# Expert passes of 104 token rows in place of 112, and a fourth round of passes in the general path

## What is computed

```
def swiglu(h, wg, wu, wd):
    return (jax.nn.silu(h @ wg) * (h @ wu)) @ wd

def moe_ffn(h, w_router, wg, wu, wd):
    hf = h.reshape(-1, D_MODEL)                      # 336 x 1024
    logits = (hf @ w_router).astype(jnp.float32)     # 336 x 8
    top_v, top_i = lax.top_k(logits, TOP_K)          # TOP_K = 2
    gates = jax.nn.softmax(top_v, axis=-1)
    ...
    out = jax.ops.segment_sum(yb * row_gate[:, None], row_tok, ...)
```

## Time and profile before

| | before |
|---|---|
| median of 3 runs | 1788.92 us (1786.96 to 1791.72) |
| the profiled execution's own time | 1789.18 us |
| its span, from first to last instruction | 1787.5 us |
| TensorE busy with matmuls | 1675.8 us (94%) |
| TensorE busy with weight loads | 1409.0 us (79%) |
| VectorE, ScalarE, GpSimd busy | 325.3, 210.5, 110.2 us |
| mean granted TensorE clock | 0.939 of full speed |
| bytes moved by DMA | 395.60 MB, mean 221 GB/s |

### The profile page before, as it was taken

One profiled execution on the slowest core, in us unless ns is written; L12 is line 12 of the kernel. 1 busy time (PEld: TensorE's weight loads), 2 busy tenths in 40 slices (PEclk: granted clock), 3 DMA queues, 4 the chain that ended last, 5 costly groups with the idle time before them and its releaser, 6 DMA issues.

```text
span 1787.5 us, 45176 instructions
## 1 busy us (share of the span) xinstructions
PE 1675.8 (94%) x20545; PEld 1409.0 (79%) x20545; DVE 325.3 (18%) x878; ACT 210.5 (12%) x603; POOL 110.2 (6%) x181
## 2 busy tenths in 40 slices
PE   3999889999999999988899999999999999999993
PEld 3767556666666766655699999999999999999993
DVE  1254631000000135552120000100000010000002
ACT  1144101000000014411010000100000000000000
POOL 6020100400000002010010000000000000000001
PEclk8999659999999999966899999999999999999997
DMA  8932112896444332211249999898998989899873
GB/s 169 265 108 86 39 39 94 292 351 230 135 111 117 97 94 66 84 50 32 90 163 341 360 314 383 305 369 325 336 371 293 375 300 360 325 339 383 283 277 103
DMA packets 211077, 395.60 MB, mean 221 GB/s; under 512 B 26466, under 2 KB 88410, under 8 KB 210736
## 3 DMA queue, kind: packets, MB, share of 16 engines
q1 hardware_dynamic: 195504, 346.83, 56.3%
q0 software_dynamic: 15152, 45.88, 8.5%
q10 hardware_dynamic: 240, 0.07, 0.0%
HBM read 357.16 MB, written 37.54 MB: 221 GB/s over the span
## 4 chain that ended last, share of the span: by engine, by line
PE 91%; DVE 4%; DMA 3%; issue 1%; ACT 1%; SPq 0%; POOLq 0%; POOL 0%; DVEq 0%
PE bank L1126 31%; PE bank L1144 15%; PE bank L1031 11%; PE bank L676 6%; PE bank L1048 6%; PE bank L1009 4%; PE bank L637 3%; DMA ring<-in_w_in 2%; PE bank L964 2%; PE bank L975 2%; PE bank L990 1%; PE bank L651 1%; PE bank L605 1%; DVE arena L1690 1%; PE bank L654 1%
## 5 line engine op out<-in xcount | busy, mean ns | idle before, releaser
L1126 PE MATMUL bank<-arena,ring 128*64 128x112 f32 x11264 | 547.3, 259 | 12.3 <-issue 12.2
L1126 PEld LDWEIGHTS bank<-arena,ring 128*64 128x64 f32 x11264 | 540.8, 137 | 17.6 <-issue 16.3
L1144 PE MATMUL bank<-arena,ring 128*64 128x112 f32 x5632 | 274.4, 259 | 1.8 <-issue 1.6
L1144 PEld LDWEIGHTS bank<-arena,ring 128*64 128x64 f32 x5632 | 271.5, 137 | 4.6 <-issue 4.1
L1031 PE MATMUL bank<-hnT,ring 128*128 128x336 f32 x704 | 199.1, 446 | 1.8 <-DVE hnT L1446 1.8
L1031 PEld LDWEIGHTS bank<-hnT,ring 128*128 128x128 f32 x704 | 133.7, 190 | 67.3 <-issue 2.3
L1827 DVE TENSOR_TENSOR arena<-arena,bank 128x112 f32<-128x112 f32 x176 | 47.7, 271 | 513.8 <-ACT arena L1400 513.8
L676 PE MATMUL bank<-hnT,ring 128*128 128x336 f32 x384 | 118.4, 453 | 0.0
L1400 ACT ACTIVATE arena<-bank 128x112 f32<-128x112 f32 x176 | 46.3, 263 | 513.5 <-PE bank L1126 513.5
L1048 PE MATMUL bank<-arena,ring 128*128 128x336 f32 x352 | 99.6, 446 | 0.0
L676 PEld LDWEIGHTS bank<-hnT,ring 128*128 128x128 f32 x384 | 70.0, 190 | 33.8 <-issue 4.6
(11 more groups left out here) (342 smaller groups left out, 1139.6 us busy)
## 6 DMA issues: line engine op xcount, KB each, us to landing
ring<-in_moe_w_gate SPq DMA_DIRECT2D x88, 1024.0 KB, 9.4
ring<-in_moe_w_up SPq DMA_DIRECT2D x88, 1024.0 KB, 8.8
ring<-in_moe_w_down SPq DMA_DIRECT2D x88, 1024.0 KB, 10.0
ring<-in_w_in SPq DMA_DIRECT2D x14, 1024.0 KB, 6.3
ring<-in_w_gate SPq DMA_DIRECT2D x11, 1024.0 KB, 12.8
ring<-in_w_up SPq DMA_DIRECT2D x11, 1024.0 KB, 11.7
xg_rows<-arena POOLq DMA_DIRECT2D x1, 11200.0 KB, 50.5
y_rows<-arena POOLq DMA_DIRECT2D x1, 10752.0 KB, 92.6
```

Source lines behind the costliest of these rows:

```text
L1126: ins = mm(bank[3 + f % 2][rows, SLOTS * w:SLOTS * w + SLOTS], weights[:, col:col + 64], xg[:, c, :], start=(c == 0), stop=(c == DK - 1))
L1144: ins = mm(bank[5 + c // 4][rows, SLOTS * (c % 4):SLOTS * (c % 4) + SLOTS], weights[:, col:col + 64], hid[:, f, :], start=(f == 0 and c % ...
```

## The change

`SLOTS` goes from 112 to 104, and `PASSES` = ceil(336 / `SLOTS`) follows from 3 to 4. Nothing else is edited.

```
-SLOTS = 112
+SLOTS = 104
 PASSES = -(-NT // SLOTS)
```

## The result

| | before | after |
|---|---|---|
| median | 1787.94 us (1785.3 to 1791.72, 4 runs) | 1812.16 us (1811.39 to 1815.6, 4 runs) |
| ratio to before | | 1.0135, 95% interval 1.0121 to 1.015 |
| profiled execution, span | 1787.5 us | 1810.1 us |

What follows compares the result with a forecast made beforehand. TensorE's expert matmuls were taken as the bound, with DMA right behind. Columns -56.3 us, holes +14 us and the rest 0 summed to -42 us against 1789.2 us, giving 1747 us, range 1731 to 1768 us.

Steps and rivals of the forecast that it cites:

- Part 1: Expert matmuls on TensorE: 8 fewer columns in each of 8448 pairs save 56.3 us; a pass without holes takes 96.2 us.
- Rival (c): Expert matmuls: the weight load, not the columns, sets 95.9 ns a pair; 1789 us, no change; chance 0.03.
- Part 2: Expert stage: the fullest expert has exactly 104 rows, so eight passes are enough and the fourth round stays unrun.
- rival (d): Expert stage: one row over 104 enters the general path, 24 more passes run, above 4000 us in all; chance 0.02.
- Part 3: TensorE in the expert stage: late program blocks come later and new ones appear, costing 14 us, bounds nothing to 25 us.
- rival (a): Expert stage: no new holes in TensorE's stream, only the column gain of 56.3 us, so 1733 us; chance 0.14.
- Part 4: Expert weight loads: bytes do not shrink, 364 GB/s needed, the ring helps; no cost taken, 30 us kept for a rival.
- Rival (b): Expert stage: DMA takes over as the bound, a pass lasts 101 us, 1753 to 1775 us in all; chance 0.18.
- Part 5: Edges of a pass and L1088: 128-column sides remain, so no gain taken, 0.3 us at most.
- Part 7: Zero fills: 5.2 MB (23%) more, landing at 437 to 494 us, before ACT's wait at 603.72 us; hidden, no cost.

## Why the prediction was wrong, point by point

**Part 1, the columns: right.** The pass without holes came out at 96.4 us (96.2 forecast) in the run with half the bytes, and 120 slots gave 110.31 (110.27 by the same law). Rival (c) is out.

**Part 2, no fourth round of passes: right.** Counts of 11264 and 5632 as before; rival (d) did not come.

**Part 3, the holes: right mechanism, wrong size.** I took 14 us with an upper bound of 25 (the formula behind it gives 23); the stage loses 65.7 in place of 21.7 us, 44 us more. The term was built as "each of the 25 late blocks is later by 0.43 us, a few new ones are added". That treats the arrival as a scatter with a tail. The rows show something near a floor: while the weights stream, a block comes every 6.2 to 6.4 us. At 112 slots TensorE used one every 6.14 us and stood close to the floor, so few holes were seen, 25. At 5.71 us there are 65, at about half of the stage's 133 block edges. Most of the edges without one follow a pass's start, where the DMA pauses (in the third pass its share is 0.11 from 1166.17 to 1170.17 us): the first 881 matmuls of that pass, nearly seven blocks, run without a hole. I had also miscounted the holes before: five of the eight passes had three or more, not six. The few holes of the kernel before looked like a small problem; they were the sign of a limit just reached. The Trainium skill, "Runtime: NRT & Kernel Launch", section "Instruction fetch mechanics", calls the cost of a block edge mostly hidden. By that, rival (a) would have come. The trace does not agree where TensorE uses a block in less than 6.3 us: 43.2 us of such waits stand in the stage after the change.

**Part 4, weights in the expert stage: right.** TensorE waits for no slab in the stage after the change, and SP still waits 496 us for TensorE. Rival (b) forecast 1753 to 1775 us by a wrong mechanism: the DMA does take gain away, but through the program blocks, not the weights. One reading in this part was loose: rows 8 show the DMA empty for 4 us, not some 8.

**Part 5, L1088: wrong by 2.2 us.** In the kernel before, the granted clock rose from half (1.2 GHz) to full (2.4 GHz) during these 48 matmuls. With 104 or 108 columns it stays at half until the stage has begun. With 112 columns and four rounds, or with 120, it rises as before. First a window of the kernel before, then two after the change, the third number from the end being the clock:

```profile
908.00:910.00 2.00, 2.00 (x20) 2.00 (x20) 0.91 (x2) 0.54 (x1) 1.43 (x2) 0.99 0.91 367
```
```profile
942.00:944.00 2.00, 2.00 (x12) 2.00 (x11) 1.44 (x3) 0.52 (x1) 1.45 (x2) 0.50 0.90 371
944.00:946.00 2.00, 2.00 (x11) 2.00 (x11) 0.00 (x0) 0.00 (x0) 1.63 (x2) 0.50 0.92 363
```

L1088 takes 9.83 us in place of 7.24. What keeps the clock down with fewer columns is not shown.

**Part 7, the fills: the step that turned the sign.** I asked who waits for the fills, found ACT at 603.72 us, and called them hidden. The landing, 171 us after its issue, was even inside what I had allowed (494 us on the clock; it came at 493). Nobody waited for it. This is the step that failed: "Hidden" was concluded from the deadline of the fills alone, and a term of 32.8 us was put at nothing. What I did not ask is who shares the DMA while they run. The feed-forward of layer 0 takes a slab of 1 MB each 9.05 us (32 matmuls of 282.8 ns), and the landing of a gate slab was already up to 53.6 us in the kernel before, against a median of 12.8. During the fills SP got out one slab each 12 us before (six from 343.28 to 416.68 us) and one each 20 us after (seven from 343.16 to 486.28 us), and so for nearly twice as long; the 11 slots of the ring, some 100 us, ran out at 437 us. The 5.2 MB more cost nothing by themselves, as the run with 112 slots and four rounds shows, and the slow layout with fewer bytes cost 5.7 us. Together they outlast the ring, and the price is 32.8 us. I had the thought that the rate might be lower by half, but used it on the landing alone.

Together: -56.3 + 44 (holes) + 32.8 (layer 0) + 2.2 (L1088) = +23 us, against 22.6 in the spans, the small rest being within what the ends of the kernel move from run to run. The fills turned the sign, but part 3 alone would have been enough to miss: with the fills over 128 partitions the kernel takes 1780.36 us, and the forecast went from 1731 to 1768.

## What to carry to other kernels

A background transfer is hidden only if those who share the DMA with it have room too: ask for its rate, how long it lasts at that rate, and its neighbours, not only for its deadline. Keep the outer dimension of a big DMA apart from tuning constants, near 128 partitions: here 104 and 120 cost about 100 GB/s against 112 and 150 against 128, and repairing that turned a kernel 1.4% slower into one 0.5 to 0.7% faster. Where an engine shows a few unexplained waits at even distances of instructions, compare its pace with the distance: if they are near each other, a faster engine will meet a floor and not a scatter.

## What was not expected of the hardware

- The DMA rate while a fill runs beside the weight loads, at a share above 1.0, by partitions of the fill: 64: 244 GB/s, 96: 346, 104: 262 to 268, 112: 365 to 370, 120: 264, 128: 414. It is the single packet that gets slower: 159 ns with 128 partitions, 281 to 289 with 104 and 120. Weight loads over 64 partitions: 220 GB/s.
- TensorE's program came in blocks of 16.4 KB, one each 6.3 us (median) beside weights at some 345 GB/s and a share of 0.95, fast enough for 5.71 us beside 192 GB/s and 0.62, and each 9.1 us beside 220 GB/s and 1.03.
- One matmul instruction of 128 output partitions put among pairs of 64 costs 181 to 186 ns more than the pair it replaces, at 104 and at 112 columns alike.
